# Head of a four-layer trunk kernel: a written-out order for the first loads, and the first norms placed between the first projection matmuls

## The reference

```python
def mixer_a(h, w_in, v_norm_g, w_s, b_s, w_out):
    u, v, z = jnp.split(h @ w_in, 3, axis=-1)
    v = rmsnorm(v, v_norm_g)
    # per chunk of 128 positions and channel group: w_s[g] (lower triangular) @ v, + b_s[g]
    y = u * mixed * jax.nn.silu(z)
    return y @ w_out

def reference(x, ...):
    for i in range(DEPTH):
        h = rmsnorm(x, norm_g[i])
        x = x + (mixer_a if i % 2 == 0 else mixer_b)(h, ...)
    return rmsnorm(x, final_g)
```

## Time and profile before

| what | before |
|---|---|
| median of 3 runs | 2098.71 us (2098.54 to 2098.89) |
| the profiled execution, its own time | 2098.52 us |
| its span on the slowest core (core 4) | 2097.0 us |
| spans of the 8 cores | 2096.0 to 2097.0 us |
| TensorE matmul busy | 2039.9 us (97%) |
| VectorE busy | 1040.8 us (50%) |
| ScalarE busy | 639.8 us (31%) |
| DMA, mean over the span | 82 GB/s |

### The profile page before, as it was taken

The page is one execution under the profiler, slowest core; times in us unless marked ns, Lnnn a source line. Parts: engine busy times, 40 slices in busy tenths (PEclk is TensorE's granted clock), DMA queues, the critical chain, the costliest instruction groups (busy, mean ns, idle before and its releaser), DMA issues.

```text
span 2097.0 us, 27850 instructions; the slowest of 8 cores (2096.0 to 2097.0 us)
## 1 busy us (share of the span) xinstructions
PE 2039.9 (97%) x9907; PEld 948.6 (45%) x9907; DVE 1040.8 (50%) x1520; ACT 639.8 (31%) x1383; POOL 84.8 (4%) x164
## 2 busy tenths in 40 slices
PE   2999999999999999999999999999999999999997
PEld 1444444444444444444444444444444444444445
DVE  2166613664555554555514663166545546465545
ACT  2811154112323213323253113511132332333222
POOL 0000000000000000000000000000000000000000
PEclk9999999999999999999999999999999999999998
DMA  9443454453444444444444444443444444455442
GB/s 238 66 81 63 79 81 69 73 96 65 81 81 78 71 74 81 79 72 72 81 81 71 71 79 71 73 80 61 81 79 72 72 81 81 71 112 119 81 81 81
DMA packets 40503, 171.81 MB, mean 82 GB/s; under 512 B 3120, under 2 KB 19632, under 8 KB 23728
## 3 DMA queue, kind: packets, MB, share of 16 engines
q0 software_dynamic: 23040, 151.01, 43.0%
q1 hardware_dynamic: 17328, 19.03, 2.9%
HBM read 312.63 MB, written 8.39 MB: 153 GB/s over the span
## 4 chain that ended last, share of the span: by engine, by line
PE 95%; ACT 2%; DMA 1%; DVE 1%; issue 1%; SPq 0%; DVEq 0%; ACTq 0%
PE bank L432 42%; PE bank L393 21%; PE bank L307 20%; PE bank L354 11%; PE bank L398 1%; DMA x_sb<-x 1%; ACT rstd L259 0%; DVE x_sb L298 0%; ACT L259 0%; ACT y_sb L279 0%; ACT sq L248 0%; PE bank L282 0%; DVE x_sb L309 0%; PE bank L268 0%; ACT rstd L261 0%
## 5 line engine op out<-in xcount | busy, mean ns | idle before, releaser
L432 PE MATMUL bank<-hT,wslot 128*128 128x512 bf16 x4096 | 886.7, 379 | 4.9 <-ACT tm L439 4.4
L432 PEld LDWEIGHTS bank<-hT,wslot 128*128 128x128 bf16 x4096 | 399.8, 98 | 490.2 <-issue 9.7
L393 PE MATMUL bank<-hT,wslot 128*128 128x512 bf16 x2048 | 462.9, 379 | 0.0
L307 PE MATMUL bank<-y_sb,wslot 128*128 128x512 bf16 (+1 forms) x2080 | 433.3, 371 | 0.0
L307 PEld LDWEIGHTS bank<-y_sb,wslot 128*128 128x128 bf16 x2080 | 204.6, 99 | 225.8
L393 PEld LDWEIGHTS bank<-hT,wslot 128*128 128x128 bf16 x2048 | 195.1, 98 | 212.4
L354 PE MATMUL bank<-wslot,hT 128*128 128x512 bf16 x1024 | 224.3, 381 | 0.0
L441 DVE TENSOR_TENSOR wx<-bank,tm 128x512 f32<-128x512 f32 x128 | 88.5, 692 | 245.9 <-PE bank L432 207.3
L401 ACT ACTIVATE tsz<-bank 128x512 f32<-128x512 f32 x128 | 76.5, 597 | 379.4 <-PE bank L393 379.4
L248 ACT ACTIVATE sq<-x_sb 128x512 f32<-128x512 f32 (+1 forms) x133 | 80.7, 607 | 320.5 <-DVE x_sb L309 320.5
L439 ACT ACTIVATE tm<-bank 128x512 f32<-128x512 f32 x128 | 76.3, 596 | 310.6 <-PE bank L432 310.6
(11 more groups left out here) (41 smaller groups left out, 843.4 us busy)
## 6 DMA issues: line engine op xcount, KB each, us to landing
wslot<-wt POOLq DMA_DIRECT2D x127, 1024.0 KB, 9.0
wslot<-wt POOLq DMA_DIRECT2D x32, 512.0 KB, 8.3
x_sb<-x SPq DMA_DIRECT2D x8, 1024.0 KB, 16.4
out<-x_sb SPq DMA_DIRECT2D x8, 512.0 KB, 3.7
out<-x_sb SPq DMA_DIRECT2D x16, 256.0 KB, 2.4
wsb_sb<-wsb SPq DMA_DIRECT2D x2, 1024.0 KB, 13.0
v_sb<-wt POOLq DMA_DIRECT2D x1, 1024.0 KB, 15.7
cst_sb<-cst SPq DMA_DIRECT2D x1, 148.0 KB, 7.3
```

Of the source, the lines that this page charges most:

```text
L307: P.add("pe", lambda e, k=k: e.matmul(banks[b][:, 0:n], lhsT=W[:, dd, k, :], rhs=y_sb[:, k, t0:t0 + n], start=(k == 0), stop=(k == KI - 1) ...
L393: P.add("pe", lambda e, bk=bk, W=W, jj=jj, m=m, k=k, t0=t0: e.matmul(banks[bk][:, :], lhsT=W[:, jj, m, k, :], rhs=hT[:, k, t0:t0 + TB], st ...
L432: P.add("pe", lambda e, bk=bk, W=W, m=m, k=k, t0=t0: e.matmul(banks[bk][:, :], lhsT=W[:, m, k, :], rhs=hT[:, k, t0:t0 + TB], start=(k == 0 ...
```

## The change

The issue order of the first loads is written out. Behind `input_x(0)` and the constants, weight tile 0 is issued at once; `input_x(1)` waits for x piece 0 to land, `input_x(2)` for the first half of weight tile 0, `input_x(3)` for x piece 1. Weight tile 1 waits for x piece 2, weight tile 2 for x piece 3. The three loads are handed to `in_proj_a` as `pre`.

Only `first_norm(0)` stands ahead of `in_proj_a` now. The other three are put before the matmuls of chunks 1, 3 and 5 of `nb` = 0, by the callback `before`.

In `out_proj_last` the list `finish` is no longer popped behind the first block of a stretch: its five steps stand behind blocks 2 to 6 where they stood behind blocks 1 to 5.

```diff
@@ out_proj_last
                         out_block(slots[dp], dd, 2 * dp + dd, p, t0, n)
-                        if finish:
+                        if finish and (dp > 0 or dd > 0):
                             finish.pop(0)()
@@ in_proj_a
-        def in_proj_a(l, base, p, hooks):
+        def in_proj_a(l, base, p, hooks, pre=(), before=None):
             la = l // 2
+            pre = list(pre)
             for nb in range(4):
-                s = load_wtile(base + nb, split=True)
+                s = pre.pop(0) if pre else load_wtile(base + nb, split=True)
                 W = wbuf[s].rearrange("p (k c) -> p k c", k=KD)
                 for tc in range(NTC):
+                    if before is not None:
+                        before(nb, tc)
                     b = next_bank()
@@ head
         input_x(0)
         P.add("sp", lambda e: e.dma_start(out=cst[:, :], in_=cst_d[:, :]), writes=(("cst",),), dsem=("cst",))
-        for q in range(1, PPP):
-            input_x(q)
-        for q in range(PPP):
-            first_norm(q)
+        head = [load_wtile(0, split=True)]
+        input_x(1, after=(("x", 0, 0),))
+        input_x(2, after=(("w", head[0], 0),))
+        input_x(3, after=(("x", 0, 1),))
+        head.append(load_wtile(1, split=True, after=(("x", 0, 2),)))
+        head.append(load_wtile(2, split=True, after=(("x", 0, 3),)))
+        first_norm(0)
+
+        def head_norm(nb, tc):
+            if nb == 0 and tc % 2 == 1 and tc < NTC - 1:
+                first_norm(tc // 2 + 1)
@@ main loop
-                    in_proj_a(l, bases[l], p, hooks)
+                    if first:
+                        in_proj_a(l, bases[l], p, hooks, pre=head, before=head_norm)
+                    else:
+                        in_proj_a(l, bases[l], p, hooks)
```

## The result

The changed kernel takes **2086.51 us** (median of 4, 2086.34 to 2086.93) against 2098.62 (median of 4, 2098.49 to 2098.89) for the kernel before: ratio 0.9942, 95% interval 0.9925 to 0.9960, so 12.1 us less where 10.1 were forecast.

The account below looks back on a forecast made before the run. TensorE, busy 1975.05 of 1980 us in the middle, was taken as the bound, leaving gains only in the head and at the end: 2098.5 - 8.2 - 1.9 = 2088.4 us, range 2083.0 to 2092.0.

Parts of the forecast that it names:

- The place of the gain: Whole kernel: nothing to win in TensorE's busy middle, only before the 64 matmuls of `nb` = 0 end and in the last 50 us.
- the head: First norms and projection: eighth bank read at 54.0 in place of 62.17 us, -8.2 us, ends -9.8 and -5.0.
- the end: Last short stretches: one L268 wait of about 2.9 us, the 0.71 gone, six blocks behind; -1.9 us.
- Loads: First loads: x piece 1 there at 19.6 to 20.6 us; weight tiles 1 and 2 in time, costed at nothing.
- The start: Head: piece 0's square stays at 8.87 us, piece 1's starts at 19.9 with up to 0.7 more.
- The cycle: Head: each norm with its two groups takes 11.2 us, between 10.5 and 12.5.
- rival 1: Head and end: the high clock holds through gaps; -11.5 and -4.3 us, time 2082.7 us; chance 0.12.
- rival 2: Head and end: every burst is cold; -2.5 and -1.8 us, time 2094.2 us; chance 0.07.
- rival 3: Head: x piece 1 lands another 4 us late, at 24; time 2092.5 us; chance 0.10.
- rival 4: Head: x piece 3 starved beside weight tile 1, landing at 60 us, say; slower, 2106.1 us; chance 0.03.

Follow-up runs that it names:

- e3: Kernel before with only the new order of the first loads, all four norms ahead of the projection, old end: 2086.50 us, ratio 0.9940.
- e11: Changed kernel with weight tiles 1 and 2 issued at once, x pieces keeping their waits: 2098.07 us, ratio 0.9993.
- e10: Changed kernel with x pieces 1 to 3 issued at once, weight tiles 1 and 2 still waiting: 2086.57 us, ratio 0.9939.
- e2: Changed kernel with the finish list back where it was, so the head's edits alone: 2088.59 us, ratio 0.9950.
- e7: e5 plus own names for the two halves of a norm's square buffer: 2080.22 us, ratio 0.9910.
- e8: e7 with groups 0 to 2 between norms on TensorE, bank reads behind the next norm, second-half x squares four groups later: 2080.83 us, ratio 0.9912.
- e9: e8 with both make_rstd of the second half of x behind the first u and z unit: 2080.81 us, ratio 0.9909.
- e12: Changed kernel with the finish list two blocks later than in the kernel before: 2085.20 us, ratio 0.9933.
- e1: Kernel before with only the finish list one block later: 2097.21 us, ratio 0.9989.
- e5: e3 and e1 together, on the kernel before: 2085.61 us, ratio 0.9936.

## Why the prediction was right, point by point

**The place of the gain** was right. The middle kept its length, the head gave 9.5 us (8.2 forecast) and the end 2.3 (1.9). That the total came within 2 us owes something to luck: in the head a late start and shorter cycles, both unforeseen, worked against each other.

**Loads.** Piece 1 was said to be there at 19.6 to 20.6; in the changed kernel ScalarE never waits for it, and in e3, where it does, the square is at 19.82 on the slowest core and from 18.4 on over the eight: the piece is there a little sooner than said. That held back weight tiles bring x early was tested by e11, that the waits between x pieces do nothing by e10. That weight tiles 1 and 2 come in time holds: no wait for them appears in TensorE's list.

**The start.** "Piece 0 has the same company as before, so its square stays at 8.87" holds only for a core: in both kernels it is early on some cores and late on others. Core 5 of the kernel before has

```profile
10.16 1.06 ACT L279 ACTIVATE y_sb<-x_sb 128x1024 bf16<-128x1024 f32 x1
```

and core 3 after 10.22. Before, this was hidden behind the wait for piece 1; now it is on the path. Cores 0, 3, 4 and 7 are late (10.2 to 10.6), and core 3, the slowest, is the only one of them on which the clock also fell at the end.

**The cycle** was the mis-sized term: 11.2 us forecast, 10.5 given as its lower end, 10.2 measured (31.52 - 21.29, 41.75 - 31.52). I had kept the norm itself at the low level in both ends. In fact the clock rose within the groups or just behind them, the first four norm matmuls ran at the high level (0.60 us for 1.01, so ScalarE waits 0.84 and not 1.25), and only then it fell. Two cycles at 1.0 us less, and a shorter last part (10.9 us from square to eighth read against 11.7), more than make up for piece 1's square being 1.4 us later than forecast: 21.29 + 2 x 10.2 + 10.9 = 52.6. One reading is off without effect: six of the seven steps from 49.90 to 62.17 are of 1.73 us, not five.

**The end.** One long wait (2.68 us for 2.9), the short one gone, six blocks behind: as said. The clock fell on four cores and for about 3.4 us on core 3, not for the 6 us seen on core 4 before, and not at all on cores 0, 2, 4 and 7. This is rival 1's course on half of the cores, but the slowest decides, so the forecast's term stood, 0.4 us low.

**The rivals.** That the clock holds through the gaps in the head (rival 1) is refuted by 1.01 us at 24.39; that every burst is cold (rival 2) by 0.60 at 22.49. The Trainium skill (TensorE: Matmul & The Clock Gate, Part 1), by which bursts with waits between can each start cold, describes the second half of each norm here, and not the first; its example has longer waits between the bursts than the norms' 1.3 and 2.4 us. Piece 1 late (rival 3) and piece 3 starved (rival 4) did not happen.

**What the prediction did not see** is that one of the change's two head edits works against the other. It costed the cycle rightly as norm plus two groups in series, but never set it against norms in series: 5.5 us each. e3 and e2 show that the interleaving costs 2.1 us once x is early. In the traces 1.5 of it is ScalarE's order: piece 1 could be squared at 19.82 (e3), but in the changed kernel the square stands behind group 0's two reads and starts at 21.29. The other 0.6 lies behind it: a group is out of the way, but each pair of groups starts at the low level again, 5.17 us for two groups where 3.5 would do at the high one. No run separates these last two. The best versions measured are e7 and the slotted ones, all near 2080.8 us or under, 6 us below the changed kernel; e7 is the simplest.

## What to carry to other kernels

When several transfers are queued at the start, ask which bytes the first computation needs and hold back everything else; here two waits on weight tiles made the whole gain of the head. Interleaving two chains on in-order engines pays only if neither's short step has to stand behind the other's: count the series both ways before mixing. A gain ahead of a saturated engine (ScalarE in e8 and e9, VectorE in e12) comes back as a wait of whoever needs it next, so move the consumers as well.

## What the runs showed of the hardware

While both queues had work, they moved the same number of packets, 153 and 153, but 0.56 and 0.16 MB: a packet of the weights carried 3.7 KB and one of x 1.0 KB (the bytes over 153), so x got a fifth of the bytes. This agrees with the Trainium skill (DMA: Bandwidth & Descriptors, Queues, rings and completion order), by which each DMA engine takes turns between queues packet by packet. Whether larger packets for x would have done what the waits do was not tried.

A wait of 2.7 us at the end dropped TensorE to half rate on four of eight cores and not on the others, with the same instructions and the same length of wait; the time of a core differed by 1.2 to 1.7 us by it. A wait of 3.5 us need not do it either: in e3 cores 1 and 6 ran on at full clock behind it and took 15.5 us to the last L268, the others 16.9 to 18.0. In the profiles of the changed kernel, e1, e5, e7, e8, e9, e10 and e11, all with the 2.7 us, two to seven cores fell, and the slowest core was one of them each time.

A third level shows too: 437 ns a matmul at a granted clock of 0.81 on cores 6 and 7 of e5 for some 13 us, while cores 4 and 5 of the same die stood at 1.00.
